# Four bank copies of ScalarE, two places further ahead in its row, in a two-layer decoder trunk

## The chip, the cores and the metric

The kernel runs on one core of a Trainium2 chip. The metric is device time in microseconds (us) of one launch. Engines named below: PE (TensorE), DVE (VectorE), ACT (ScalarE), POOL (GpSimd) and SP (SyncE, which here only issues DMAs). Each engine works through its own list of instructions in order; semaphores hold an instruction back until another engine or a DMA has counted up.

## The reference, cut to what matters

The residual stream x is 256 tokens by 2048 features in float32. Layer 0 is a block-sparse attention layer, layer 1 an mLSTM layer. Both have this frame:

```python
mod = cond @ ada_w[layer] + ada_b[layer]          # 2048 -> 3 * 2048, one row
shift, scale, gate = jnp.split(mod, 3, axis=-1)
h = rms_norm(x, norm_w[layer]) * (1.0 + scale) + shift
y = branch(h, ...)                                # in-projection, mixer, * silu(z), out-projection
x = x + gate * y
```

The in-projection of layer 0 is `h @ w_in` with 2048 rows and 4 x 2048 columns (q, k, v, z). `h` needs scale and shift, and these need the whole of `ada_w`'s 2048 rows. With 256 tokens the weights are the traffic: some 360 MB are read in one launch.

## The kernel before, in words

**Float32 by three products.** Each weight piece of 256 rows by 512 columns (512 KB; called a *granule*, numbered in order of use) is loaded into `raw`, one of five slots. ACT rounds it into `w_hi` (`hi`, line 592), DVE subtracts the rounded part and gets `w_lo` (`lo`, line 873), and PE adds up `w_hi*h_hi + w_lo*h_hi + w_hi*h_lo`: 12 matmuls of 512 columns a granule (lines 1418 to 1420). The five slots are the LEAD: granule c's `hi` waits for the load of c and for PE to have finished granule c - 5 (`granule_used`), and SP issues the load of c only when DVE has done `lo` of c - 5 (`lo_ready`). SP issues all loads of this stage, in one order, on one queue.

**The first block.** `h` is not ready all at once. Scale and shift come in four quarters of 512 features. Each quarter is the sum over 16 tiles of `ada_w` of 512 KB, each multiplied and added on DVE (`take_ada`, line 892, output `ada_acc`), then summed over partitions by 16 small matmuls on PE (`mod_sum`, line 1562), and brought to `scale_c` and `shift_c` by DVE (`mod_evac`, line 911); after that ACT and DVE make the quarter's `h_hi` and `h_lo` (`h_make`, lines 647 and 652; `h_rest`, line 955). The sums k = 1 and k = 2 stand behind granules 10 and 21. So that PE has work meanwhile, layer 0 starts with granules that need only the first quarters of `h`: `BLOCKS0` is a hand-written order. Granules 0 to 13 use the first quarter, 14 to 23 the second, 24 to 39 the third.

**Parts.** Four products (z of the first three head groups and v of the second) are summed in parts, since no PSUM bank is free long enough. Such a part is a run of two or more granules into the bank pair `mixes[1]`. When the first run is done (granules 3, 6, 9 and 13 end them), ACT copies the bank to SBUF: `z_copy(act, j, c)` waits for granule c on PE and then takes a 128 x 1024 copy (line 659). These are the *four copies*; the table `Z_COPIES` holds (j, c) = (0, 3), (1, 6), (2, 9), (3, 13). Later runs are added to the copy by DVE (`z_add`, line 918), at the places of `Z_ADDS`. PE waits for them before it writes the bank again (`claim0`): granule 5 for copy 0, granule 8 for copy 1, the sum k = 1 for copy 2, granule 12 for `mod_evac` of k = 1, granule 16 for copy 3, granule 19 for the first `z_add`, and granule 29 for the third.

**The order on ACT and DVE** is set by `run`: at place i it does the tasks of the table `first` for i, then prepares granule i + 5 (`hi` or `lo`), then the tasks of the other table for i. Copy j stands in ACT's `first`. In DVE's tables `take_ada` is spread over the places by `TAKES0`, `mod_evac` of k = 1 and k = 2 stand behind `lo` of granules 15 and 26, `h_rest` at places 11, 12 and 22, 23, and the first three `z_add` in front of `lo` of granules 22, 25 and 32. On ACT, `h_make` of the second quarter stands behind `hi` of 15, that of the third behind `hi` of 26.

Of the kernel before, what the change touches and what calls it, by code (L numbers as in the profile page):

```python
# [121 lines left out]
def build(nc, x, c, norm_w, ada_w, ada_b, att_w_in, att_q_norm, att_k_norm, att_w_out,  # L122
# [12 lines left out]
    with ctx:  # L135
# [257 lines left out]
        Z_COPIES = ((0, 3), (1, 6), (2, 9), (3, 13))  # L393
# [36 lines left out]
        def late0(g):  # L430


            return 1 if g == 1 else 0
# [160 lines left out]
        def squares(act, layer, q):  # L594

            if layer == 0:
                act.wait_ge(x_in[q], 16)
            elif q == CHUNKS - 1:
                act.wait_ge(tile_out, 1)
            else:  # L600
                act.wait_ge(x1_chunk, q + 1)
            for t in range(1 if layer and q == CHUNKS - 1 else NT):
                act.activation(xn[:, t, q * NC:(q + 1) * NC], stream[:, t, q * NC:(q + 1) * NC],
                               ACT.Square, scale=float(D) ** -0.5, accum_out=xsq[:, t, q:q + 1]
                               ).then_inc(xsq_ready, 1)

        def norm_act(act, layer):

            act.wait_ge(xrs_step, layer + 1)
            for q in range(CHUNKS):  # L610
                if layer == 1 and q > 1:
                    h_make(act, 1, 2 * (q - 2))
                    h_make(act, 1, 2 * (q - 2) + 1)
                act.activation(xn[:, 0, q * NC:(q + 1) * NC], stream[:, 0, q * NC:(q + 1) * NC],
                               ACT.Copy, scale=xrs[:, 0:1]).then_inc(xn_act, 1)
# [8 lines left out]
        def xnT_evac(act, q):  # L624

            act.wait_ge(ht_done, q + 1)
            act.activation(xnT[:, 2 * q:2 * q + 2, :].rearrange("p k s -> p (k s)"), turn_bank(0, q)[:], ACT.Copy
                           ).then_inc(xnT_act, 1)
# [6 lines left out]
        def h_make(act, layer, q):  # L635


            act.wait_ge(mod_out, q // 2 + 1 if layer == 0 else 2 * CHUNKS)
            if layer:
                act.wait_ge(ht_done, UNIT + q + 1)  # L640
            else:
                act.wait_ge(xnT_act, q + 1)
            wait(act, h_ready, UNIT * layer + q - 1)
            for k in range(2):
                kt = 2 * q + k
                src = turn_bank(layer, q)[:, k * SEQ:(k + 1) * SEQ] if layer else xnT[:, kt, :]
                op = act.activation(h_hi[:, kt, :], src, ACT.Identity, scale=scale_c[:, layer, kt:kt + 1],
                                    bias=shift_c[:, layer, kt:kt + 1])
                if by_both(layer, q):
                    op.then_inc(h_act, 1)  # L650
                    continue
                act.activation(h_full[:, q % 2, k * SEQ:(k + 1) * SEQ], src, ACT.Identity,
                               scale=scale_c[:, layer, kt:kt + 1],
                               bias=shift_c[:, layer, kt:kt + 1]).then_inc(h_act, 1)

        def z_copy(act, j, c):

            act.wait_ge(granule_used, c + 1)
            act.activation(parts[j], mixes[1][:], ACT.Copy).then_inc(z_copied, 1)
# [7 lines left out]
        def q_evac(act, g, c):  # L667
            wait(act, s0_done, g)
            qk_evac(act, g, 0, c)
# [14 lines left out]
        def vz_evac(act, g, u, c, dst, func=ACT.Copy):  # L684

            act.wait_ge(granule_used, c + 1)
            act.activation(dst, pair0(u, g, UNIT - 1)[:], func).then_inc(in_evac, 1)
# [111 lines left out]
        def merged(*tables):  # L799
            out = {}  # L800
            for t in tables:
                for i, tasks in t.items():
                    out.setdefault(i, []).extend(tasks)
            return out
# [4 lines left out]
        def act_program(act):  # L809
            act.dma_start(rows_c, c[0].rearrange("(t p) -> t p", p=P)).then_inc(c_in, 16)  # L810
            act.dma_start(const[:], consts[:, 0:C_COS]).then_inc(consts_in, 16)
            act.dma_start(rows_n, norm_w.rearrange("l (t p) -> (l t) p", p=P)).then_inc(c_in, 16)
            act.dma_start(rows_v, mlstm_norm_w[0].rearrange("(t p) -> t p", p=P)).then_inc(rows_in, 16)
            act.dma_start(conv_rows, mlstm_conv_w[0].rearrange("k (j p) -> (k j) p", p=P)).then_inc(rows_in, 16)
            act.wait_ge(consts_in, 16)
            act.activation(mask_b[:], const[:, C_MASK:C_MASK + P], ACT.Copy)
            act.activation(ident_b[:], ident, ACT.Copy).then_inc(masks_ready, 1)
            act.wait_ge(rows_turned, 1)
            act.activation(cond[:], proj[1][0][:, 0:KT], ACT.Silu).then_inc(cond_ready, 1)
            for q in range(CHUNKS):  # L820
                squares(act, 0, q)
            norm_act(act, 0)

            for q in range(UNIT):
                xnT_evac(act, q)
            layer0 = merged(
                {-5: [lambda: h_make(act, 0, 0)], -4: [lambda: h_make(act, 0, 1)]},
                {i: [lambda b=b: h_make(act, 0, 2 * b), lambda b=b: h_make(act, 0, 2 * b + 1)]
                 for i, b in SUM_AFTER.items()},
                {41: [lambda: q_evac(act, 0, 41)], 43: [lambda: qk_evac(act, 0, 1, 43)],  # L830
                 45: [lambda: vz_evac(act, 0, V_, 45, v0)], 51: [lambda: qkT_evac(act, 0)],
                 54: [lambda: exp0(act, 0)], 58: [lambda: pT0_evac(act, 0)], 60: [lambda: z_silu(act)],
                 65: [lambda: y_hi_act(act, 0)], 68: [lambda: gates_hi(act)]},
                *[{GROUP0[g] + 7: [lambda g=g: q_evac(act, g, GROUP0[g] + 7)],
                   GROUP0[g] + 15: [lambda g=g: qk_evac(act, g, 1, GROUP0[g] + 15)],
                   GROUP0[g] + late0(g) + 20: [lambda g=g: qkT_evac(act, g)],
                   GROUP0[g] + late0(g) + 23: ([] if g == 1 else [lambda g=g: vz_evac(act, g, V_, GROUP0[g] + 23, v0)])
                   + [lambda g=g: exp0(act, g)],
                   GROUP0[g] + late0(g) + 27: [lambda g=g: pT0_evac(act, g)]} for g in range(1, G0)],
                {GROUP0[1] + 35: [lambda: y_hi_act(act, 1)], GROUP0[2] + 34: [lambda: y_hi_act(act, 2)],  # L840
                 GROUP0[3] + 31: [lambda: vz_evac(act, 3, Z_, GROUP0[3] + 31, z0[3], ACT.Silu)],
                 GROUP0[3] + 34: [lambda: y_hi_act(act, 3, None, y_hi_last)]},
                {LAST0 + 2 * q + 3: [lambda q=q: squares(act, 1, q)] for q in range(CHUNKS - 2)},
                gate_tasks(lambda bank, b: gate_evac(act, bank, b), SUM_GATE0, 0))
            run(act, hi, 0, 0, NG0, layer0, -LEAD, merged(
                {i: [lambda j=j, i=i: z_copy(act, j, i)] for j, i in Z_COPIES},
                {NG0 - 1: [lambda q=q: squares(act, 1, q) for q in (CHUNKS - 2, CHUNKS - 1)]}))
            norm_act(act, 1)
            for q in range(4, UNIT):
                h_make(act, 1, q)  # L850

            run(act, hi, 0, NG0, HEAD, merged(
                {8: [lambda: gates_evac(act), lambda: gates_log(act)], 12: [lambda: floor_exp(act)]},
                act_group1(act, 0, 0, NG0),
                gate_tasks(lambda bank, b: gate_evac(act, bank, b), SUM_GATE1, CHUNKS)))
            run(act, hi, 0, NG0 + HEAD, BODY, merged(
                {1: [lambda: y_hi_act(act, G0, 0)]}, act_group1(act, 1, 0, NG0 + HEAD),
                gate_tasks(lambda bank, b: gate_evac(act, bank, b), SUM_GATE1, CHUNKS + 2)))
            with act.Fori(1, H1 - 2) as it:
                run(act, hi, it, NG0 + HEAD, BODY, merged(  # L860
                    {1: [lambda: y_hi_act(act, it + G0, it)]}, act_group1(act, it + 1, it, NG0 + HEAD)))
            it = H1 - 2
            run(act, hi, it, NG0 + HEAD, BODY, merged(
                {1: [lambda: y_hi_act(act, it + G0, it)],
                 34: [lambda: y_hi_act(act, G0 + H1 - 1, H1 - 1, y_hi_last)]},
                act_group1(act, H1 - 1, it, NG0 + HEAD)))
            run(act, hi, 0, NG0 + HEAD + (H1 - 1) * BODY, UNIT - LEAD, {})
# [999 lines left out]
```

## Time and profile before

| | us |
|---|---|
| median of 3 runs | 1507.15 (1506.7 to 1507.38) |
| the profiled execution's own time | 1510.35 |
| its span, first to last instruction | 1508.5 |
| PE busy in the span | 1460.5 (97%) |
| DVE busy | 1103.9 (73%) |
| ACT busy | 745.3 (49%) |

All times inside the program below are counted from the span's start. The first granule starts on PE at 41.33 us; layer 0 ends near 556 us. The TensorE clock that was granted is 0.990 of full on average: it stood at half in a few short stretches.

### The profile page before, as it was taken

Reading aid. Unit: us, or ns where it says so; the run is one execution under the profiler, and the core shown is the slowest. Engines: PE = TensorE matmul, PEld = TensorE weight load, DVE = VectorE, ACT = ScalarE, POOL = GpSimd, SP = SyncE. Lnnn points to the kernel's source line nnn. Section 1 sums busy time; section 2 is a strip of 40 time slices with the busy share of each in tenths; the row PEclk is TensorE's granted clock in tenths of the full one; section 3 lists DMA queues with packets and bytes.
Section 4 is the critical chain, followed back from the end, with each engine's and each line's share of the span. In section 5 each row is a group of like instructions: output and inputs, shape, how many; then the busy total and the mean of one; then the engine's idle time right before and its main releaser. Section 6 shows DMA issues by size and latency. Waiting matters only on the chain.

```text
span 1508.5 us, 19084 instructions
## 1 busy us (share of the span) xinstructions
PE 1460.5 (97%) x6692; PEld 1207.1 (80%) x6692; DVE 1103.9 (73%) x1237; ACT 745.3 (49%) x1002; POOL 42.7 (3%) x80
## 2 busy tenths in 40 slices
PE   5989999999999989999999999999999999999998
PEld 4767878888888867778888888888888888888887
DVE  5998898989898885877866566566666656656657
ACT  4544546455445455645544544554454554454452
POOL 0000010101000000000000000000000000000000
PEclk9999999999999999999999999999999999999999
DMA  9999889997989745798756556566566556556653
GB/s 348 386 386 384 272 283 323 320 345 278 325 297 354 268 126 182 242 316 296 259 178 188 174 190 188 173 194 182 172 191 193 167 187 192 177 181 195 181 182 113
DMA packets 198630, 361.47 MB, mean 240 GB/s; under 512 B 14268, under 2 KB 47508, under 8 KB 198568
## 3 DMA queue, kind: packets, MB, share of 16 engines
q1 hardware_dynamic: 197848, 359.23, 72.3%
q0 software_dynamic: 304, 1.06, 0.2%
q8 instruction: 37, 0.61, 0.2%
q10 hardware_dynamic: 416, 0.37, 0.1%
q14 instruction: 25, 0.20, 0.0%
HBM read 358.51 MB, written 2.11 MB: 239 GB/s over the span
## 4 chain that ended last, share of the span: by engine, by line
PE 59%; DVE 2%; issue 1%; ACT 1%; POOL 0%; ACTq 0%; DVEq 0%
PE proj L1418 19%; PE proj L1419 18%; PE proj L1420 18%; PE mix L1687 1%; DVE ada_acc L892 1%; PE mix L1418 1%; PE mix L1419 1%; PE mix L1420 1%; PE mix L1639 0%; DVE w_lo L873 0%; PE mix L1663 0%; DVE work L1135 0%; PE mix L1580 0%; PE mix L1693 0%; PE mix L1538 0%
## 5 line engine op out<-in xcount | busy, mean ns | idle before, releaser
L873 DVE TENSOR_TENSOR w_lo<-raw,w_hi 128x1024 fp32r<-128x1024 f32 x480 | 585.6, 1222 | 356.5 <-ACT w_hi L592 356.3
L592 ACT ACTIVATE w_hi<-raw 128x1024 fp32r<-128x1024 f32 x480 | 507.7, 1062 | 685.0 <-PE proj L1420 575.2
L1418 PE MATMUL proj<-w_hi,h_hi 128*128 128x512 f32 x1472 | 584.9, 397 | 3.4 <-DVE w_lo L873 2.0
L1420 PE MATMUL proj<-w_hi,h_lo 128*128 128x512 f32 x1472 | 575.5, 391 | 0.0
L1419 PE MATMUL proj<-w_lo,h_hi 128*128 128x512 f32 x1472 | 575.3, 391 | 0.0
L1418 PEld LDWEIGHTS proj<-w_hi,h_hi 128*128 128x128 f32 x1472 | 277.9, 189 | 64.0 <-issue 6.1
L1420 PEld LDWEIGHTS proj<-w_hi,h_lo 128*128 128x128 f32 x1472 | 277.5, 189 | 58.9
L1419 PEld LDWEIGHTS proj<-w_lo,h_hi 128*128 128x128 f32 x1472 | 277.8, 189 | 58.2 <-issue 2.0
L892 DVE SCALAR_TENSOR_TENSOR ada_acc<-ada_raw,cond,ada_acc 128x1024 f32<-128x1024 f32 x147 | 187.7, 1277 | 5.1 <-DMA ada_raw<-in_ada_w 3.9
L1418 PE MATMUL proj<-w_hi,y_hi 128*128 128x512 f32 x320 | 125.9, 394 | 1.3 <-DVE stream L1053 1.3
L1420 PE MATMUL proj<-w_hi,y_lo 128*128 128x512 f32 x320 | 124.6, 389 | 0.0
L1419 PE MATMUL proj<-w_lo,y_hi 128*128 128x512 f32 x320 | 124.6, 389 | 0.0
L1418 PEld LDWEIGHTS proj<-w_hi,y_hi 128*128 128x128 f32 x320 | 60.1, 188 | 14.3 <-DVE stream L1053 1.5
L1419 PEld LDWEIGHTS proj<-w_lo,y_hi 128*128 128x128 f32 x320 | 60.1, 188 | 12.7 <-issue 0.5
L1420 PEld LDWEIGHTS proj<-w_hi,y_lo 128*128 128x128 f32 x320 | 60.1, 188 | 12.6
L1418 PE MATMUL mix<-w_hi,h_hi 128*128 128x512 f32 x128 | 51.0, 398 | 6.7 <-issue 6.7
L1420 PE MATMUL mix<-w_hi,h_lo 128*128 128x512 f32 x128 | 50.4, 393 | 0.0
L1419 PE MATMUL mix<-w_lo,h_hi 128*128 128x512 f32 x128 | 50.3, 393 | 0.0
L1135 DVE SCALAR_TENSOR_TENSOR work<-work,conv_c 128x256 f32<-128x256 f32 x96 | 39.9, 475 | 0.0
L1059 DVE TENSOR_TENSOR ada_raw<-proj,gate 128x1024 f32<-128x1024 f32 x31 | 37.7, 1217 | 2.6 <-PE proj L1420 2.6
L1062 DVE TENSOR_TENSOR stream<-ada_raw,stream 128x1024 f32<-128x1024 f32 x31 | 38.0, 1225 | 1.1
L1418 PEld LDWEIGHTS mix<-w_hi,h_hi 128*128 128x128 f32 x128 | 24.6, 192 | 13.5 <-issue 8.5
(221 smaller groups left out, 960.4 us busy)
## 6 DMA issues: line engine op xcount, KB each, us to landing
raw<-in_mlstm_w_in SPq DMA_DIRECT2D x192, 512.0 KB, 3.7
ada_raw<-in_ada_w SPq DMA_DIRECT2D x160, 512.0 KB, 6.3
raw<-in_att_w_in SPq DMA_DIRECT2D x128, 512.0 KB, 7.4
raw<-in_mlstm_w_in SPq DMA_DIRECT2D x128, 256.0 KB, 3.0
raw<-in_mlstm_w_out SPq DMA_DIRECT2D x64, 512.0 KB, 4.2
raw<-in_att_w_out SPq DMA_DIRECT2D x32, 512.0 KB, 5.9
ada_more<-in_ada_w SPq DMA_DIRECT2D x16, 512.0 KB, 11.4
work<-in_ada_w SPq DMA_DIRECT2D x16, 512.0 KB, 11.3
```

The source lines that it names most:

```text
L592: act.activation(w_hi[:, c % LEAD, :], raw[:, c % LEAD, :], ACT.Copy).then_inc(hi_ready, 1)
L873: dve.tensor_tensor(w_lo[:, c % LEAD, :], raw[:, c % LEAD, :], w_hi[:, c % LEAD, :].bitcast(F32), ALU.subtract).then_inc(lo_ready, 1)
L892: dve.scalar_tensor_tensor(out=sum_, in0=w, scalar=cond[:, t:t + 1], in1=other, op0=ALU.mult, op1=ALU.add).then_inc(ada_tile, 1)
L1059: dve.tensor_tensor(scaled, both[q % 2][:], gate_both(q), ALU.mult).then_inc(out_part, 1)
L1062: dve.tensor_tensor(x_q, scaled, x_q, ALU.add).then_inc(out_evac, 1)
L1135: op = dve.scalar_tensor_tensor(out=cv[:, j, :], in0=src, scalar=w, in1=cv[:, j, :], op0=ALU.mult, op1=ALU.add)
L1418: pe.matmul(out_, a_hi, b_hi, start=start, stop=False, **kw)
L1419: pe.matmul(out_, a_hi, b_lo, start=False, stop=False, **kw)
L1420: return pe.matmul(out_, a_lo, b_hi, start=False, stop=stop, **kw)
L1687: op = pe.matmul(mix[0][:, a:b], cv[:, j, q], cv[:, 2 + j, 0:b - a], start=(j == 0), stop=(j == 1))
```

## The change

In the table `first` of ACT's run over layer 0 each copy moves from place c to place c - 2. What the copy waits for and what it does stay the same.

```diff
             run(act, hi, 0, 0, NG0, layer0, -LEAD, merged(
-                {i: [lambda j=j, i=i: z_copy(act, j, i)] for j, i in Z_COPIES},
+                {i - 2: [lambda j=j, i=i: z_copy(act, j, i)] for j, i in Z_COPIES},
                 {NG0 - 1: [lambda q=q: squares(act, 1, q) for q in (CHUNKS - 2, CHUNKS - 1)]}))
```

On ACT's list, copy 0 stood in front of `hi` of granule 8 and now stands in front of `hi` of 6; copy 1 moves from 11 to 9, copy 2 from 14 to 12, and copy 3 from 18 to 16.

## Rows read from the trace of the kernel before

**Rows 1.** Page, DMA issues: issue, KB each, median us from issue to landing

```profile
raw<-in_mlstm_w_in SPq DMA_DIRECT2D x192, 512.0 KB, 3.7
```

**Rows 2.** Windows: length, busy us (count) by engine, granted clock, DMA share, GB/s

```profile
100.00:120.00 20.00, 16.35 (x75) 13.46 (x74) 18.22 (x19) 6.37 (x6) 0.00 (x0) 0.95 1.05 384
```

**Rows 3.** Waits of PE, 41 to 130 us: total, times, longest

```profile
PE mix L1418 <- issue: 6.7, 4, 2.8
PE mix L1562 <- DVE ada_acc L892: 3.3, 2, 2.1
```

**Rows 4.** Waits of PE, 125 us to the end: the longest one

```profile
PE mix L1538 <- ACT work L614: 4.1, 1, 4.1
```

**Rows 5.** Timeline of PE: start, length, instruction, [idle before, releaser]

```profile
53.36 0.39 PE L1418 MATMUL proj<-w_hi,h_hi 128*128 128x512 f32 x1
...
57.53 0.47 PE L1418 MATMUL mix<-w_hi,h_hi 128*128 128x512 f32 x1 [1.28 <-issue]
...
66.99 0.47 PE L1418 MATMUL mix<-w_hi,h_hi 128*128 128x512 f32 x1 [1.03 <-issue]
...
76.68 1.92 PE L1562 MATMUL mix<-ones,ada_acc 128*128 128x1 f32 x16 [1.26 <-DVE ada_acc L892]
...
84.23 0.77 PE L1418 MATMUL mix<-w_hi,h_hi 128*128 128x512 f32 x1 [2.76 <-issue]
...
106.50 0.47 PE L1418 MATMUL mix<-w_hi,h_hi 128*128 128x512 f32 x1 [1.58 <-issue]
...
117.00 2.73 PE L1562 MATMUL mix<-ones,ada_acc 128*128 128x1 f32 x16 [2.06 <-DVE ada_acc L892]
...
124.80 0.40 PE L1418 MATMUL mix<-w_hi,h_hi 128*128 128x512 f32 x1
...
141.13 0.47 PE L1418 MATMUL mix<-w_hi,h_hi 128*128 128x512 f32 x1
```

**Rows 6.** Timeline of ACT: hi (L592), copies (L659), h_make (L647)

```profile
56.42 1.00 ACT L659 ACTIVATE work<-mix 128x1024 f32<-128x1024 f32 x1
...
70.32 1.06 ACT L592 ACTIVATE w_hi<-raw 128x1024 fp32r<-128x1024 f32 x1 [1.64 <-DMA raw<-in_att_w_in]
...
88.12 1.05 ACT L592 ACTIVATE w_hi<-raw 128x1024 fp32r<-128x1024 f32 x1
...
91.35 1.03 ACT L659 ACTIVATE work<-mix 128x1024 f32<-128x1024 f32 x1 [0.48 <-PE mix L1420]
...
92.52 1.06 ACT L592 ACTIVATE w_hi<-raw 128x1024 fp32r<-128x1024 f32 x1
...
100.63 1.06 ACT L592 ACTIVATE w_hi<-raw 128x1024 fp32r<-128x1024 f32 x1 [1.63 <-DMA raw<-in_att_w_in]
...
109.60 1.06 ACT L592 ACTIVATE w_hi<-raw 128x1024 fp32r<-128x1024 f32 x1 [2.52 <-PE mix L1420]
...
120.03 0.60 ACT L647 ACTIVATE h_hi<-stream,shift_c,scale_c 128x256 fp32r<-128x256 f32 x1 [3.70 <-DVE scale_c L911]
...
125.06 1.06 ACT L592 ACTIVATE w_hi<-raw 128x1024 fp32r<-128x1024 f32 x1 [0.98 <-PE proj L1420]
```

**Rows 7.** Timeline of DVE: take_ada (L892), lo (L873), z_add (L918)

```profile
75.25 1.28 DVE L892 SCALAR_TENSOR_TENSOR ada_acc<-work,cond,ada_acc 128x1024 f32<-128x1024 f32 x1
...
82.76 1.23 DVE L873 TENSOR_TENSOR w_lo<-raw,w_hi 128x1024 fp32r<-128x1024 f32 x1 [0.23 <-ACT w_hi L592]
...
89.19 1.23 DVE L873 TENSOR_TENSOR w_lo<-raw,w_hi 128x1024 fp32r<-128x1024 f32 x1 [1.88 <-ACT w_hi L592]
...
105.18 1.21 DVE L918 TENSOR_TENSOR work<-mix,work 128x1024 f32<-128x1024 f32 x1
...
126.15 1.23 DVE L873 TENSOR_TENSOR w_lo<-raw,w_hi 128x1024 fp32r<-128x1024 f32 x1 [1.58 <-ACT w_hi L592]
...
139.81 1.21 DVE L918 TENSOR_TENSOR gate<-mix,gate 128x1024 f32<-128x1024 f32 x1
```

**Rows 8.** Timeline of SP: the load of granule 21

```profile
90.45 0.37 SPq L455 DMA_DIRECT2D raw<-in_att_w_in  x1
```

## The prediction

> **What bounds the kernel now.** Start with the windows view by stage. Between 100 and 120 us DMA is full (384 GB/s) and DVE is busy 18.22 of 20 us, while PE, the bound of the whole span, is busy only 16.35 [rows 2]. So in this stage PE waits. The waits of PE show for what: from 41 to 130 us it stood 6.7 us in four waits that the view can only call "issue", at matmuls that write `mix`, and 3.3 us in two waits for `ada_acc` [rows 3]. After 130 us it hardly waits: the longest wait is 4.1 us at the border of the layers [rows 4]. PE's timeline places the six: granule 5 (1.28), granule 8 (1.03), the sum k = 1 (1.26), granule 12 (2.76), granule 19 (1.58), the sum k = 2 (2.06) [rows 5]. From 124.80 to 141.13 six granules take 16.33 us, 2.72 each, with no wait: that is PE's pace, and from there on whatever comes late is carried to the end. The question is therefore when granule 29, at 141.13, starts after the change.
>
> Who ends each wait: granules 5 and 8 start 1.1 us after copies 0 and 1 begin (56.42 to 57.53). Granule 12 waits for `mod_evac`, which stands behind DVE's `lo` of 15 (82.76, ends 83.99), itself behind a load. Granule 19 at 106.50 follows the first `z_add` (105.18 + 1.21 = 106.39), and granule 29 the third (139.81 + 1.21 = 141.02) [rows 5, 7].
>
> **Copies 0, 1 and 2.** No instruction is added or removed. Copy 0 today stands behind `hi` of 7, which waits for its load; it runs at 56.42 although granule 3 was done when granule 4 started at 53.36. Now it runs at about 53.36 + 0.2 = 53.56, granule 5 starts at the pace, 56.08 for 57.53, and granule 8 follows at 64.24 for 66.99 (copy 1 at 61.7). Granule 10 ends at 64.24 + 3 x 2.72 = 72.40; before, with 1.26 idle ahead of 76.68, it ended at 75.4. So the two waits, 2.3 us, are gone and PE is 3 us ahead.
>
> That lead buys nothing. The sum k = 1 waits for the sixteenth `take_ada`, at 75.25 on DVE [rows 7], which is fed by full DMA queues. It may even be a little later: `hi` of 12, at 70.32, now stands behind copy 2, which waits for granule 9 (69.68 + 0.2), and with 1.17 us from a waiting copy to the next `hi` (91.35 to 92.52 [rows 6]) it starts at 71.05, 0.7 late; `hi` of 6 and 9 are late too, but DVE reaches their `lo` no earlier than before. Granule 12 then waits for `lo` of 15 as before and starts at 84.23. The gain is 0; its bounds are 0 and, should nothing hold these two gates, 3.6 (the two waits and the 1.26 of the third).
>
> **Copy 3 costs.** Today `hi` of 16 runs at 88.12, straight behind `h_make`, and `hi` of 17 behind it, two granules before granule 13 is done; copy 3 follows at 91.35 [rows 6]. Now copy 3 stands in front of both and waits for granule 13. Behind it on ACT are `hi` of 16, 17 and 18; behind `hi` of 16 is DVE's `lo` of 16 (89.19), and behind that, in DVE's order, everything else.
>
> When is granule 13 done? Before, 84.23 to 91.35 is 7.12 us for two granules and the wake-up of ACT, where the pace gives 5.44 + 0.20: 1.48 us went to the low clock (the first matmul there shows 0.77 us [rows 5], the level is 1.2 GHz in place of 2.4). After, PE stands still earlier and longer, 72.40 to about 77, so the clock falls during that wait and is back while granule 11 is worked, hidden before 84.23. I take granule 12 at the full clock: copy 3 starts at 84.23 + 5.64 = 89.87, `hi` of 16 at 91.04, 2.92 us later than 88.12. If the clock is low as before, copy 3 stays at 91.35 and `hi` of 16 starts at 92.52, 4.4 us late: the upper bound. The lower bound is 2.75: the copy can't start before granule 13 ends, and takes 1.00 us.
>
> DVE has no gap from 89.19 to 116 us (18.22 of 20 busy in rows 2, the rest being the gap behind it), so the 2.92 us pass on: first `z_add` 108.10 for 105.18, granule 19 at 109.42 for 106.50. PE reaches it at 89.67 + 5 x 2.72 = 103.27 and stands 6.15 us. What hides the loads: `raw` of 21 is issued at 90.45 and used at 100.63 [rows 8, 6]; issued 2.92 later at 93.37, it has 7.3 us left where a load without a queue takes 3.7 [rows 1]. SP's other loads of the stage are behind it and as late. The cover holds, so the DMAs add nothing.
>
> **The clock behind it.** In the trace the granted clock fell in or after waits of 2.76 and 2.06 us; a wait of 6.15 will do the same. At the low level sum and granule took 117.00 to 124.80, 7.80 us, where 1.92 + 2.72 = 4.64 is the price at the high one; the sum's share is 2.73 - 1.92 = 0.81, so a whole granule costs 2.35 more. For granule 19 I take 1.5, close to the 1.48 behind 84.23 (bounds 0 and 2.35). It ends at 113.64, and `hi` of 24, which waits for it (109.60 before [rows 6]), starts at 113.9, 4.3 late; its `lo` had 0.3 to spare. DVE is then 4.0 late, and so is the sum k = 2: 121.0 for 117.00.
>
> PE's wait in front of this sum is now 121.0 - (113.64 + 5.44) = 1.9 us, between the 1.58 at granule 19 that left the clock up and the 2.06 that took it down. Clock down: everything is 4.0 late, as before plus the shift. Clock up: `h_make` starts 3.03 - 0.81 = 2.22 us behind the sum's start (before 120.03 - 117.00 = 3.03), at 123.2, and leaves ACT 4.05 us later (125.06 - 0.98 = 124.08 before), so `hi` of 27 is at 127.3 for 125.06: 2.2 late. `lo` of 27 follows it (126.15), and from there to the third `z_add` DVE has no gap: granule 29 is 2.2 or 4.0 late. PE itself would be ready sooner (125.64 for 124.80), so DVE decides. I take the middle, 3.1 us.
>
> A rule of the Trainium skill bears on the width, not on the sum: the page "TensorE: Matmul & The Clock Gate", Part 1, says that the gate's measuring runs free and is not reset when a kernel starts, so that the same kernel may lose different numbers of matmuls to it. By that rule the two outcomes above would alternate between runs; the three timed runs lie within 0.7 us, which shows little of it.
>
> **Sum.** 0 (copies 0 to 2) + 2.92 (copy 3) + 1.1 (clock behind granule 19) - 0 or 1.8 (clock at the sum) = 4.0 or 2.2, taken as 3.1. The profiled execution goes from its own 1510.35 (span 1508.5) to 1513.5; it lies 3.2 above the median of the runs, 1507.15, and the same difference put on that gives 1510.3 us.
>
> **The rivals.** *The clock gives the delay back.* If granule 19 and the sum both ran at the full level, the sum would start at 117.00 + 2.92 = 119.92, `hi` of 27 at 119.92 + 2.22 + 4.05 = 126.2, 1.1 late: 1508.3, within 0.2%. For it: the low clock at the sum cost 3.16 us before, which is there to be won. Against it: the 6.15 us wait. Chance 0.24, with smaller absorptions anywhere.
> *The lead is kept (faster).* Place: the sum k = 1 and granule 12. If the takes came as early as PE does, 3.6 us of lead would last and DVE, too, would be early at the first `z_add`. It decides from the point where `take_ada` of 75.25 moves to 72.4 or before. Time 1507.15 - 3.6 = 1503.6. Against it: full DMA, and DVE's order. Chance 0.08.
> *The DMA cover breaks.* Loads issued 3 to 4 us late leave the queues dry, and a second delay of that size (2.92) is added: 1513.2. Against it: 7.3 us against 3.7. Chance 0.06.
> *The forecast's mechanism:* 0.62.
>
> A measurement tells from no change what is over 0.2%, 3.0 us here. The forecast's 0.62 splits around that bound: some 0.20 below 3.0, 0.42 above, for 2.2 to 4.0 stretch to 5.4 if copy 3 stays at 91.35 (4.4 and more). Slower is 0.42 + 0.06 = 0.48, same 0.20 + 0.24 = 0.44, faster 0.08. The range, 1507.6 to 1512.6, leaves out most of the two outer rivals and the edge of the first.
>
> **What would show it.** Right: no wait at granules 5 and 8; sum k = 1 still near 76.7 to 77.1, granule 12 near 84.2; copy 3 near 89.9 with `hi` of 16 directly behind it near 91.0; granule 19 near 109.4 behind a wait of about 6 us; granule 29 between 143.3 and 145.1. Wrong: `hi` of 16 near 88, granule 19 at or before 106.5, or granule 29 late by 2 us and more while the end is not.

## The result, and the profile after

The changed kernel takes 1512.86 us (median of 6 runs, 1511.78 to 1514.37), the kernel before on the same chip 1507.56 us (1506.7 to 1508.78, 6 runs). The ratio is 1.0038, with a 95% interval of 1.0027 to 1.0048: 5.3 us slower. The forecast was 1510.3 with a range up to 1512.6. The direction was right, the size was not.

The page of the changed kernel shows the same instructions in the same number, and hardly a trace of the loss (columns: busy us, share of the span, count):

```profile
span 1509.9 us, 19084 instructions
PE 1460.7 (97%) x6692; PEld 1207.5 (80%) x6692; DVE 1104.4 (73%) x1237; ACT 744.9 (49%) x1002; POOL 43.4 (3%) x80
```

The waits of PE from 41 to 130 us do show it (total, times, longest). Six waits of 10.0 us in all [rows 3] have become three of 12.7:

```profile
PE mix L1562 <- DVE ada_acc L892: 7.0, 2, 5.4
PE mix L1418 <- issue: 5.7, 1, 5.7
```

PE's timeline places them. These rows answer to [rows 5]: granules 5 and 8 with no wait, the sum k = 1, granules 11, 12, 19 and 20, the sum k = 2, granules 23 and 29.

```profile
55.15 0.39 PE L1418 MATMUL mix<-w_hi,h_hi 128*128 128x512 f32 x1
...
63.31 0.39 PE L1418 MATMUL mix<-w_hi,h_hi 128*128 128x512 f32 x1
...
76.99 3.54 PE L1562 MATMUL mix<-ones,ada_acc 128*128 128x1 f32 x16 [5.36 <-DVE ada_acc L892]
...
80.40 0.77 PE L1418 MATMUL mix<-w_hi,h_hi 128*128 128x512 f32 x1
...
85.64 0.40 PE L1418 MATMUL mix<-w_hi,h_hi 128*128 128x512 f32 x1
...
110.63 0.77 PE L1418 MATMUL mix<-w_hi,h_hi 128*128 128x512 f32 x1 [5.75 <-issue]
...
115.89 0.59 PE L1418 MATMUL mix<-w_hi,h_hi 128*128 128x512 f32 x1
...
123.31 1.92 PE L1562 MATMUL mix<-ones,ada_acc 128*128 128x1 f32 x16 [1.60 <-DVE ada_acc L892]
...
129.15 0.63 PE L1418 MATMUL mix<-w_hi,h_hi 128*128 128x512 f32 x1
...
145.90 0.39 PE L1418 MATMUL mix<-w_hi,h_hi 128*128 128x512 f32 x1
```

The waits at 57.53 and 66.99 are gone and PE is 3.7 us ahead at granule 8 (0.9 us of it was there at granule 4 already, 52.43 for 53.36, before any copy could act). It then stands 5.4 us in front of the sum k = 1, which starts at 76.99 for 76.68. Granule 12 is 1.4 us late, granule 19 4.1, granule 29 4.8 (145.90 for 141.13).

On ACT (answers to [rows 6]) copy 3 now waits 3.30 us for PE, and four `hi` stand behind it, that of 16 first, at 92.25 for 88.12:

```profile
91.32 1.03 ACT L659 ACTIVATE work<-mix 128x1024 f32<-128x1024 f32 x1 [3.30 <-PE mix L1420]
...
92.25 3.89 ACT L592 ACTIVATE w_hi<-raw 128x1024 fp32r<-128x1024 f32 x4
...
100.36 1.06 ACT L592 ACTIVATE w_hi<-raw 128x1024 fp32r<-128x1024 f32 x1 [1.58 <-DMA raw<-in_att_w_in]
...
116.19 1.06 ACT L592 ACTIVATE w_hi<-raw 128x1024 fp32r<-128x1024 f32 x1 [9.26 <-PE mix L1420]
```

On DVE (answers to [rows 7]) `lo` of 16 comes 4.14 us later than 89.19, after a gap of 6.2 us, and the first `z_add` is 4.13 us later than 105.18; in the third row, the third `z_add` is 4.41 later than 139.81:

```profile
93.33 1.23 DVE L873 TENSOR_TENSOR w_lo<-raw,w_hi 128x1024 fp32r<-128x1024 f32 x1 [6.20 <-ACT w_hi L592]
...
109.31 1.22 DVE L918 TENSOR_TENSOR work<-mix,work 128x1024 f32<-128x1024 f32 x1
...
144.22 1.22 DVE L918 TENSOR_TENSOR gate<-mix,gate 128x1024 f32<-128x1024 f32 x1
```

SP issues the load of granule 21 at 94.58 for 90.45 [rows 8], and `hi` of 21 still starts at 100.36, where it was 100.63. No load came late.

One number of the two pages can mislead: the spans differ by 1.4 us only, 1509.9 and 1508.5. Each page is one execution. That of the kernel before took 1510.35 us, above the median of its runs by 2.8, and that of the changed kernel, 1511.78, was the fastest of its six. One thing that differs between executions is where the granted clock falls. Here are windows of both (length, busy us and count of PE, PEld, DVE, ACT and POOL, then granted clock, DMA share and GB/s), first the kernel before:

```profile
620.00:632.00 12.00, 9.55 (x44) 7.69 (x44) 12.00 (x14) 5.74 (x7) 0.00 (x0) 1.00 0.78 254
640.00:652.00 12.00, 9.68 (x36) 7.57 (x35) 9.92 (x10) 3.39 (x6) 2.40 (x6) 0.86 1.02 366
```

and the changed one:

```profile
620.00:632.00 12.00, 9.55 (x38) 7.51 (x37) 12.00 (x16) 5.02 (x5) 0.64 (x1) 0.86 0.89 285
640.00:652.00 12.00, 11.33 (x50) 9.03 (x49) 11.53 (x12) 5.13 (x9) 2.31 (x4) 1.00 0.98 336
```

In layer 1 the low stretch sits at 643.5 to 647 us in the one and at 628 to 632 us in the other. The lag of a matmul behind the same matmul of the kernel before (at these times of the kernel before) is 4.8 us at granule 29, 3.6 from 255 us on, 3.1 at 568 us, 4.6 at 628 us, behind the low stretch of the changed kernel, and 1.4 from 647 us on, behind that of the kernel before. The low stretch is as long in both but costs 1.6 us in its one place and 3.2 in the other. What comes and goes in layer 1 goes with the place of these stretches in the two executions; nothing in it points to the change.

### The profile page after: what moved, and what is told of

Its sections match the earlier page's. It is cut to its first block, busy times and chain, and to the rows that moved or that the text cites. A ratio compares the mean times of both kernels' runs of the same rounds, so it can differ in the third digit from the quotient of the medians.

```text
span 1509.9 us, 19084 instructions
## 1 busy us (share of the span) xinstructions
PE 1460.7 (97%) x6692; PEld 1207.5 (80%) x6692; DVE 1104.4 (73%) x1237; ACT 744.9 (49%) x1002; POOL 43.4 (3%) x80
## 4 chain that ended last, share of the span: by engine, by line
PE 59%; DVE 2%; issue 1%; ACT 1%; POOL 0%; ACTq 0%; DVEq 0%
PE proj L1418 18%; PE proj L1420 18%; PE proj L1419 18%; PE mix L1687 1%; DVE ada_acc L892 1%; PE mix L1418 1%; PE mix L1419 0%; PE mix L1420 0%; PE mix L1639 0%; DVE w_lo L873 0%; PE mix L1663 0%; DVE work L1135 0%; PE mix L1580 0%; PE mix L1538 0%; PE mix L1693 0%
## 5 line engine op out<-in xcount | busy, mean ns | idle before, releaser
L873 DVE TENSOR_TENSOR w_lo<-raw,w_hi 128x1024 fp32r<-128x1024 f32 x480 | 586.0, 1223 | 359.6 <-ACT w_hi L592 359.3
L592 ACT ACTIVATE w_hi<-raw 128x1024 fp32r<-128x1024 f32 x480 | 507.4, 1061 | 686.3 <-PE proj L1420 584.2
L892 DVE SCALAR_TENSOR_TENSOR ada_acc<-ada_raw,cond,ada_acc 128x1024 f32<-128x1024 f32 x147 | 187.8, 1278 | 5.0 <-DMA ada_raw<-in_ada_w 3.8
L1419 PEld LDWEIGHTS proj<-w_lo,y_hi 128*128 128x128 f32 x320 | 60.1, 188 | 12.7 <-issue 0.5
```

What stands on the lines that cost most here:

```text
L592: act.activation(w_hi[:, c % LEAD, :], raw[:, c % LEAD, :], ACT.Copy).then_inc(hi_ready, 1)
L873: dve.tensor_tensor(w_lo[:, c % LEAD, :], raw[:, c % LEAD, :], w_hi[:, c % LEAD, :].bitcast(F32), ALU.subtract).then_inc(lo_ready, 1)
L892: dve.scalar_tensor_tensor(out=sum_, in0=w, scalar=cond[:, t:t + 1], in1=other, op0=ALU.mult, op1=ALU.add).then_inc(ada_tile, 1)
L1419: pe.matmul(out_, a_hi, b_lo, start=False, stop=False, **kw)
```

## The experiments

Each kernel was run beside the kernel before, whose median was 1507.17 to 1507.78 us in these batches, so kernels are compared by their ratios. The table gives the median, the ratio to the kernel before with its interval, and from the one profiled execution the start of `hi` of 16 on ACT and of granules 12, 19 and 29 on PE.

| kernel | median us | ratio (95%) | hi 16 | g 12 | g 19 | g 29 |
|---|---|---|---|---|---|---|
| before | 1507.56 | 1 | 88.12 | 84.23 | 106.50 | 141.13 |
| b2, before again | 1507.99 | 1.0002 (0.9994 to 1.0011) | 88.04 | 84.59 | 106.42 | 139.45 |
| f1, before + take ahead | 1507.34 | 0.9999 (0.9990 to 1.0008) | 88.12 | 84.45 | 105.55 | 138.57 |
| e2, copies 0 to 2 only | 1507.31 | 1.0002 (0.9992 to 1.0012) | 87.49 | 85.26 | 105.87 | 138.95 |
| e3, copy 3 by one place | 1507.95 | 1.0000 (0.9991 to 1.0010) | 87.96 | 84.07 | 106.34 | 141.24 |
| e4, the wait alone | 1511.68 | 1.0028 (1.0019 to 1.0038) | 89.78 | 84.04 | 108.17 | 143.42 |
| e1, copy 3 only | 1511.91 | 1.0029 (1.0020 to 1.0038) | 90.82 | 84.17 | 109.20 | 143.51 |
| e5b, change + 5 dummies | 1511.57 | 1.0029 (1.0017 to 1.0042) | 90.96 | 84.31 | 109.35 | 144.32 |
| the change | 1512.86 | 1.0038 (1.0027 to 1.0048) | 92.25 | 85.64 | 110.63 | 145.90 |
| a2, the change again | 1512.62 | 1.0034 (1.0021 to 1.0047) | 93.06 | 86.25 | 111.45 | 146.36 |
| f2, change + take ahead | 1510.29 | 1.0020 (1.0012 to 1.0029) | 92.94 | 85.95 | 109.94 | 144.30 |
| e5, change + 18 dummies | 1518.39 | 1.0078 (1.0063 to 1.0092) | 97.23 | 90.67 | 115.62 | 149.85 |

**Which copy costs.** e1 moves only copy 3, e2 only the other three, e3 only copy 3 and by one place.

```diff
-                {i: [lambda j=j, i=i: z_copy(act, j, i)] for j, i in Z_COPIES},
+                {i - 2 * (j == 3): [lambda j=j, i=i: z_copy(act, j, i)] for j, i in Z_COPIES},   # e1
+                {i - 2 * (j < 3): [lambda j=j, i=i: z_copy(act, j, i)] for j, i in Z_COPIES},    # e2
+                {i - (j == 3): [lambda j=j, i=i: z_copy(act, j, i)] for j, i in Z_COPIES},       # e3
```

> Only copy 3 moves (place 13 to 11); copies 0 to 2 stay. Theory W (the wait of copy 3 in front of hi of 16 makes DVE late): granule 13 ends as in the kernel before, copy 3 at about 91.3 us, hi of 16 at 92.4 (4.3 us late), granule 19 near 110.8, granule 29 some 4 to 5 us late; the time rises by 4 to 5.5 us, as for the whole change. Rival C (the earlier copies 0 to 2 let PE stand, the clock falls, and that is the cost): no loss without them, 0 to 1 us. Rival D (loads issued too late): as W in the total, but hi of 20 to 23 would start later than 97.9, 100.6, 103.3 and 106.0 us.

> Copies 0 to 2 move, copy 3 stays at place 13. Theory W: waits at granules 5 and 8 are gone, PE stands some 5 us in front of the sum k = 1, the clock falls, granule 12 starts between 84.2 and 85.7, but hi of 16 stays at 88.1 and granule 19 at 106.5: the time moves by -0.5 to +1 us. Rival C: most of the loss, 3 to 5 us. Rival 'lead kept': 2 to 3 us faster.

> Only copy 3 moves, and by one place (13 to 12), so it stands in front of hi of 17 and behind hi of 16. Theory W: hi of 16 at 88.1 as before, hi of 17 at about 92.4 in place of 89.8, but DVE reaches lo of 17 only at 93.5 (two takes and one h_rest stand ahead of it), so nothing is late: -0.5 to +0.7 us. If any earlier copy 3 costs by the place (half of the loss for one place), 2 to 2.7 us slower.

e1 costs 0.29% (4.4 us by its ratio), e2 and e3 nothing that can be measured. So copy 3 carries the loss, and only the second of its two places. ACT's timeline of e1 shows the copy waiting for PE with three `hi` behind it:

```profile
89.89 1.03 ACT L659 ACTIVATE work<-mix 128x1024 f32<-128x1024 f32 x1 [1.73 <-PE mix L1420]
...
90.82 2.94 ACT L592 ACTIVATE w_hi<-raw 128x1024 fp32r<-128x1024 f32 x3
```

In e3 `hi` of 16 is on time and only that of 17 is late, at 90.75 for 89.81, where DVE has work of its own until 93.5:

```profile
87.96 1.04 ACT L592 ACTIVATE w_hi<-raw 128x1024 fp32r<-128x1024 f32 x1
...
89.83 1.03 ACT L659 ACTIVATE work<-mix 128x1024 f32<-128x1024 f32 x1 [0.82 <-PE mix L1420]
...
90.75 1.05 ACT L592 ACTIVATE w_hi<-raw 128x1024 fp32r<-128x1024 f32 x1
```

In e1's and e3's profiled executions granule 12 ran at the full clock, so copy 3 started near 89.9 and not at 91.3 as e1's expectation had it; the time it gave held.

**The wait or the copy.** e4 leaves all copies in place and adds one wait.

```diff
+                {11: [lambda: act.wait_ge(granule_used, 14)]},
```

> The kernel before, all four copies in their old places, and one wait added on ScalarE in front of hi of 16: for granule 13 on PE. Theory W: hi of 16 starts at about 91.4, 3.3 us late (no copy of 1 us behind the wait), granule 19 at about 109.8, and the time rises by 2.5 to 4.5 us, a little less than for copy 3 alone. If the cost is the copy's own microsecond or its bank, and not the wait, the time stays within 1 us.

4.2 us slower by its ratio, as much as e1 within the intervals. The copy's own microsecond and its bank are not needed for the loss. Here `hi` of 16 was only 1.7 us late in the profiled execution (89.78). The rest came behind granule 19: it waited 4.83 us and then ran at the low clock, so that granule 20 started at 113.43 for 109.34, 4.1 us late. Granule 29 was 2.3 us late against the first trace and 4.0 against b2's.

**What copies 0 to 2 add.** With all four copies moved PE stands still in front of the sum k = 1, and the clock falls. e2 shows the same (a wait of 5.45 us, the sum in 3.55 us, granule 12 at 85.26) and costs nothing, since its `hi` of 16 doesn't wait for granule 13. e5 and e5b fill that wait with matmuls into a free bank.

```diff
             pe.wait_ge(bank_sem, count)
+            if sum_ is mod_sum and args == (1,):
+                for _ in range(18):                       # e5; range(5) in e5b
+                    pe.matmul(mix[2][:], ident, const[:], start=True, stop=True)
             sum_(pe, *args)
```

> The changed kernel once more, on the same chip as the next three. All theories: 4 to 6 us above the kernel before. Theory W+ (the cost is DVE's delay behind copy 3's wait alone, some 4.5 us; what copies 0 to 2 add is the fall of the clock in front of granule 11, 0 to 1.5 us, in some executions): hi of 16 between 91.0 and 92.6 us.

> The changed kernel, and on PE 18 dummy matmuls of 512 columns into a free bank, between the wait for copy 2 and the wait for the takes of the sum k = 1: about 4 us of work in a stretch in which PE stands still otherwise. Theory W+: the clock stays up over granule 11, granule 12 starts at 84.2 in every execution and copy 3 near 89.9, so hi of 16 is at 91.0: 0 to 1.5 us faster than the changed kernel, still 3 to 5 us above the kernel before. If the clock in front of granule 11 is the main cost, all of the loss goes.

> The changed kernel with 5 dummy matmuls in place of 18 in the wait in front of the sum k = 1. A dummy takes 0.87 us (two passes of 0.43: 36 records in 15.61 us with 18 of them), so 5 fill 4.3 us of the wait of 5.4 to 6.1. Theory W+: the sum near 77 in 1.9 us, granule 12 at 84.2 to 84.5, copy 3 near 89.9, hi of 16 near 90.9; 0.5 to 1.5 us faster than the changed kernel, still 3.5 to 5 us above the kernel before. If the clock in front of granule 11 is the main cost, within 1 us of the kernel before.

e5 missed its aim: a float32 matmul of 512 columns is two records of 0.43 us each, so the dummies filled 15.61 us in place of 4. It turned into another useful run, one in which everything is later: granule 13 is done at 96.1, `hi` of 16 starts at 97.23, 9.1 us late, granule 29 is 8.7 us late, and the time is 11.8 us longer by its ratio. e5b fits the wait. PE's timeline (dummies, sum, granules 11 and 12):

```profile
71.99 4.45 PE L1648 MATMUL mix<-const 128*128 128x512 f32 x10
...
77.16 1.95 PE L1562 MATMUL mix<-ones,ada_acc 128*128 128x1 f32 x16 [0.72 <-DVE ada_acc L892]
...
78.97 0.48 PE L1418 MATMUL mix<-w_hi,h_hi 128*128 128x512 f32 x1
...
84.31 0.47 PE L1418 MATMUL mix<-w_hi,h_hi 128*128 128x512 f32 x1 [0.76 <-issue]
```

Without the dummies the sum took 3.54 us and granule 12 started at 85.64; with them 1.95 us and 84.31, and `hi` of 16 is at 90.96 in place of 92.25 and 93.06. The dummies did not keep the clock up for good: it fell inside granule 11, from 80 to 83 us (granted clock 0.50; 80.43 to 82.99 the matmuls stand 0.43 us apart). But there it was over before granule 12, and granule 12's own wait, 0.76 us, hid it. In the changed kernel it was low from 75.3 to 85.6 us. So the trace shows that working PE in the wait takes away the delay of granule 12; its worth in time (1511.57 against 1512.86 and 1512.62, some 1 us) is within the intervals of the ratios, and not shown.

**The loss is DVE's order.** f1 and f2 move one of DVE's two takes at place 11 to place 10, ahead of `lo` of 16, f1 in the kernel before, f2 in the changed one. The line below is f1's and f2's, in `takes0`.

```diff
-            spans = ((-LEAD, 14, KT), (9, 2, 5), (11, 10, 11), (21, 2, 5), (23, 13, 11), (40, 103, 6 * KT))
+            spans = ((-LEAD, 14, KT), (9, 2, 6), (11, 10, 10), (21, 2, 5), (23, 13, 11), (40, 103, 6 * KT))
```

> The kernel before with its copies in place, and one of DVE's two takes of place 11 moved to place 10, so that it runs in DVE's gap in front of lo of 16 (1.88 us before) and not behind it; SP's load of that tile moves along. Theory W (what stands on DVE between lo of 16 and the third z_add decides when granule 29 starts): that stretch is 1.28 us shorter, granule 19 and the sum k = 2 start 1.2 us earlier, 0.5 to 1.5 us faster. If the stage is bound by loads or by PE: within 0.5 us.

> The changed kernel with the same take moved in front of lo of 16, where DVE now has a gap of 6.2 us. Theory W: 1.2 us less than the changed kernel. If the loss is not DVE's: no difference to the changed kernel.

f2 is at 1510.29, 2.3 us below the changed kernel on the same chip (1512.62), in the profiled executions with `hi` of 16 at the same place (92.94 and 93.06) and granule 19 1.5 us sooner (109.94 and 111.45). The two intervals overlap a little (up to 1.0029, and from 1.0021), and part of the gain is clock: granule 19, behind a wait of 4.36 us in place of 5.75, took 4.41 us in place of 5.26. The 1.5 us in front of granule 19 are as forecast from DVE's order: what stands on DVE behind `lo` of 16 decides when granule 19 starts. f1 gave 1507.34, ratio 0.9999 (0.9990 to 1.0008): no gain that can be told, though its trace has granule 19 at 105.55, 1 us sooner. Whether a gain of 0.5 to 1 us is there stays open.

**The reference itself.**

> The kernel before, once more, for a second trace of it: no change in the time. If the profiled execution that the prediction was worked out from had an unusual amount of low clock (sum k = 2 and granule 22 wholly at the low level), this one shows less of it: the sum k = 2 in 1.9 us in place of 2.7, and granule 29 at 139 to 140 us. If its clock was usual, granule 29 starts at 141 us again.

The time is the same. In this second trace of the kernel before, the sum k = 2 takes 1.92 us, not 2.73, and granule 29 starts at 139.45 (granule 23 at 123.12 for 124.80):

```profile
106.42 0.47 PE L1418 MATMUL mix<-w_hi,h_hi 128*128 128x512 f32 x1 [2.27 <-issue]
...
116.92 1.92 PE L1562 MATMUL mix<-ones,ada_acc 128*128 128x1 f32 x16 [2.07 <-DVE ada_acc L892]
...
118.70 0.48 PE L1418 MATMUL proj<-w_hi,h_hi 128*128 128x512 f32 x1
```

At the sum k = 1 the same trace shows something else: behind a wait of 0.99 us the clock fell during the sum, and granule 11 ran low as in the changed kernel:

```profile
77.14 2.33 PE L1562 MATMUL mix<-ones,ada_acc 128*128 128x1 f32 x16 [0.99 <-DVE ada_acc L892]
...
79.32 0.77 PE L1418 MATMUL mix<-w_hi,h_hi 128*128 128x512 f32 x1
```

f1 and the second run of f3 (below) have it too, behind waits of 1.27 and 1.26 us. A low clock in granule 11 is therefore not the mark of the long wait. What the four traces with a wait of 4.87 us and more (the change, a2, e2, f2) have alone is that the whole sum was low as well, so that granule 12 came at 85.26 to 86.25; in all others but e5 it came at 84.04 to 84.59.

**A version that is likely faster than both.** f3 keeps the copies where they were and brings the takes of the sum k = 2 forward.

```diff
+            spans = ((-LEAD, 14, KT), (9, 2, 6), (11, 9, 10), (21, 2, 5), (23, 13, 11), (40, 103, 6 * KT))
```

> The kernel before with its copies in place; of the 16 takes of the sum k = 2, one more ahead of lo of 16 and the last ones one place sooner (they end at place 19, ahead of the second z_add and of lo of 25, not at 20). Theory W: the sum k = 2 no longer waits for DVE's order; it starts 2 us sooner and granule 29 1 to 2 us sooner: 0.5 to 2 us faster. If loads bound it there, the raw loads that the takes' loads now go ahead of cost as much: within 0.5 us.

> The same kernel as f3 once more, to narrow its interval (the first gave 0.9993, 0.9984 to 1.0001). If the sum k = 2 at the pace of PE is worth what the trace shows (granule 29 at 139.4 us with the low clock behind granule 19, granule 23 at 121.2), 0.5 to 1.5 us faster than the kernel before again. If the first result was chance: within 0.5 us.

f3 gave 1506.18 us, ratio 0.9993 (0.9984 to 1.0001), and again 1505.18 us, ratio 0.9986 (0.9977 to 0.9995). In its second trace the sum k = 2 waits 0.22 us in place of 2.06 and starts at 114.68 (in its first, at 116.64 with no wait, since granule 19 had run at the low clock, and granule 29 came at 139.39, as in b2's, 139.45):

```profile
106.02 0.47 PE L1418 MATMUL mix<-w_hi,h_hi 128*128 128x512 f32 x1 [2.49 <-issue]
...
114.68 1.95 PE L1562 MATMUL mix<-ones,ada_acc 128*128 128x1 f32 x16 [0.22 <-DVE gate L918]
...
116.48 0.47 PE L1418 MATMUL proj<-w_hi,h_hi 128*128 128x512 f32 x1
```

The second interval lies below 1, the first reaches 1: a gain of 1 to 2 us, small but likely, on a place the change did not touch.

## Why the prediction was wrong in size

**Copies 0 to 2 gain nothing: right.** The waits at granules 5 and 8 went, the lead was lost at the sum k = 1 (76.99; 76.7 to 77.1 was said), and e2 measured 1.0002.

**Copy 3 makes `hi` of 16 late: right, and mis-sized.** The term was 2.92 us, with granule 12 at 84.23 and at the full clock. In the changed kernel it was 4.13 (92.25), and 4.94 in a2. The first step that failed is the sentence that the clock "is back while granule 11 is worked, hidden before 84.23". The whole sum ran at the low level, 3.54 us, and so did granule 11, 5.24 us from 80.40 on; granule 12 could start only at 85.64. e1, with copy 3 moved alone, has no such long wait (0.98 us): granule 12 at 84.17, copy 3 at 89.89, `hi` of 16 at 90.82, granule 19 at 109.20. The prediction's numbers were 84.23, 89.87, 91.04 and 109.42, and its 121.0 for the sum k = 2 was 120.98 in e1. The chain was right, its starting point was not. What I gave as the upper bound of this term, 4.4, lies between what the two traces of the changed kernel show.

**DVE passes it on, DMA hides the loads: right.** First `z_add` 4.13 late, granule 19 4.13 late, wait of 5.75 (6.15 forecast); `hi` of 21 on time.

**The clock behind granule 19: right in kind, mis-sized.** I took 1.5 us for the low clock in that granule. From 110.63 to 115.89 it took 5.26 us, 2.5 over the pace of 2.72, more than the upper bound of 2.35. That bound was worked out a little low: it takes 1.92 us for the sum at the full level, but from the sum's start to the next matmul it is 1.78 (76.68 to 78.46), which gives 2.49. So `hi` of 24 came at 116.19 (6.6 late) and the sum k = 2 6.3 late, where 4.3 and 4.0 were forecast. This is the second step that failed. All seven traces with `hi` of 16 late (granule 19 waits 4.36 to 5.75 us) show the low clock in granule 19; of the seven others two do, e3 behind 2.95 us and the first of f3 behind 3.19, so that the clock there is not the change's alone.

**The clock at the sum k = 2: the term that should not have been there.** I subtracted up to 1.8 us because a sum at the full clock would be cheaper than the 2.73 us of before. It was (1.92). But b2 shows the sum of the kernel before at 1.92 as well, with a time that is no lower than usual. e2 and f1, too, have it at 1.92. The credit was taken from one execution that had lost more to the clock at this place than the others, though not more over the whole span (granted clock 0.990 in both traces of the kernel before), and the median of the runs does not have it to give. Against b2's trace the changed kernel is 6.45 us late at granule 29 (145.90 and 139.45), against the first trace 4.77; the measured 5.3 lies between. e1 bears this out: its granule 29 came at 143.51, where the prediction has 143.3 with the clock up, and yet it cost 4.4 us and not 2.4.

With the terms as measured, the sum is 4.13 + 2.5 (granule 19) - 0.3 (the slack of `lo` of 24) = 6.3 us, near the 6.45 against b2's trace; the first term was 4.94 in a2 and 2.70 in e1. That is an account made afterwards, not a test, and it ends at granule 29. How the lag there becomes the 5.3 of the medians stays open: tested are the cause (e1, e4), the part that is free (e2, e3), the path over DVE (f2), and the delay of granule 12 by the clock (e5b), this last in one trace only.

**From granule 29 everything late is carried to the end: not wholly.** In the changed kernel 1.1 us of the lag is gone again at 255 us (4.7 to 3.6 against the first trace), where PE stood 0.60 us in the kernel before; in a2 and e1 it is 0.7. The prediction had no term for this.

The rivals: the clock did not give the delay back, the lead was not kept (e2), and the DMA cover held (`hi` of 21 at 100.36 for 100.63).

## What to carry to other kernels

An instruction that waits must be judged by what stands behind it in its queue. Copy 3 moved two places: the first was free, since DVE reached that granule later anyway, and the second cost 4 to 5 us, since `hi` of 16 was the one that a gap on DVE was waiting for. Look for the row where the next engine shows idle time, and put nothing that waits in front of what it waits for.

Freeing a bank sooner is worth nothing when PE's next gate hangs on another engine, and a longer wait in one piece can cost more than the same time in pieces: in all four traces with one of 4.87 us and more before the sum k = 1 the whole sum ran at the low clock, 3.5 us in place of 1.9, and in none with waits near 1 us. Short waits are no guarantee, as b2's 0.99 us shows. And it cost time only where something later waited for it (the change, but not e2).

A profiled execution is one draw. Before a difference of a few microseconds is credited to the clock, its stretches have to be read in a second trace of the same kernel.

## What the runs showed of the hardware that was not expected

The spread between runs is as large as the effect: in one batch of 33 runs the kernel before took from 1504.43 to 1510.25 us. Its two traces differ in where the granted clock falls: at the sum k = 2, 2.73 us, its later part at the low level, in one and 1.92 at the full level in the other, after waits of the same length (2.06 and 2.07 us). The Trainium skill's page "TensorE: Matmul & The Clock Gate", Part 1, says that the gate's measuring is not tied to a kernel's start; these two rows agree with that, but do not show the cause.

After the 5.4 us wait in the changed kernel the 16 small matmuls of the sum took 3.54 us in place of 1.92, and the clock stayed low through the granule behind them; where e5b had kept PE working with matmuls of 512 columns ahead of the sum, it stayed up through the sum (1.95 us) and fell in the granule behind it.

At the full clock a float32 matmul of 512 columns into one bank cost 0.87 us (e5, 36 records in 15.61 us for 18 of them), against 0.23 us from one to the next of the rounded kind (2.72 us for 12).
